# Expert rows summed in HBM by accumulating DMAs from POOL, combine stages that read the sums, and first gathers issued in the router stage

## The reference, cut to what matters

```python
# block 1
for e in range(N_EXPERTS):
    hid = jax.nn.silu(t @ w_gate[e]) * (t @ w_up[e])
    out = out + combine[:, e:e + 1] * (hid @ w_down[e])
x = x + gate2 * out
# block 2, for the tokens `toks` of expert e
hb = x_pad[toks] @ w1[e] + b1[e]
g_part = jnp.minimum(hb[..., ::2], SWIGLU_LIMIT)
u_part = jnp.clip(hb[..., 1::2], -SWIGLU_LIMIT, SWIGLU_LIMIT)
act = g_part * jax.nn.sigmoid(SWIGLU_ALPHA * g_part) * (u_part + 1)
y = act @ w2[e] + b2[e]
out = zeros.at[slot_tok].add(y * slot_gate)
```

## Time and profile before

| | us |
|---|---|
| median of 3 runs | 2692.19 (2686.52 to 2699.84) |
| the profiled execution, its own time | 2694.49 |
| its span, first to last instruction | 2692.7 |
| router stage 1 up to the last index, starts 562, ends | 604.8 |
| expert stage 1, up to the last copy of its products | 867.0 |
| combine stage 1, starts 871.2, ends | 903.7 |
| router stage 2, up to the last index | 1617.9 |
| expert stage 2, up to the last copy of its products | 2627.5 |
| combine stage 2, starts 2631.7, ends with the span | 2692.7 |

### The profile page before, as it was taken

How to read it: one execution, slowest core, us unless ns; L and a number is a source line. 1 busy time by engine, 2 the same in 40 slices (tenths; PEclk the granted TensorE clock), 3 DMA queues, 4 the chain that set the end, 5 groups by cost and what they waited for, 6 DMA issues and landing times. The chain is left out here.

```text
span 2692.7 us, 33335 instructions
## 1 busy us (share of the span) xinstructions
PE 2428.8 (90%) x12618; PEld 1168.4 (43%) x12618; DVE 1036.6 (38%) x2285; ACT 490.2 (18%) x1140; POOL 224.4 (8%) x248
## 2 busy tenths in 40 slices
PE   7999878968886899999999978999899998999975
PEld 3445656534443455667544432333233342333323
DVE  4856564761111655467421153222122222132215
ACT  3232441021111311255111020000000000000003
POOL 0000000001101000068200001000000000000002
PEclk9997777989997999899999989999999999999995
DMA  8534302669998600010311067999999999999994
GB/s 341 217 125 174 124 1 95 256 283 368 418 384 348 229 32 4 32 63 33 116 61 47 1 265 301 413 419 419 420 418 385 417 419 419 419 418 418 419 386 162
DMA packets 144054, 691.33 MB, mean 257 GB/s; under 512 B 14860, under 2 KB 42508, under 8 KB 78344
## 3 DMA queue, kind: packets, MB, share of 16 engines
q1 hardware_dynamic: 120776, 635.19, 58.4%
q0 software_dynamic: 9376, 31.73, 3.1%
q10 hardware_dynamic: 13744, 22.30, 2.3%
HBM read 640.14 MB, written 49.02 MB: 256 GB/s over the span
## 5 line engine op out<-in xcount | busy, mean ns | idle before, releaser
L2029 PE MATMUL bank<-ring,ex_xt 128*64 128x512 f32 (+4 forms) x2240 | 359.2, 507 | 25.8 <-DMA ring<-in_up 23.3
L2029 PE MATMUL bank<-x_spare,ex_xt 128*64 128x512 f32 (+4 forms) x1504 | 270.6, 519 | 18.1 <-DMA x_spare<-in_up 17.1
L2029 PEld LDWEIGHTS bank<-ring,ex_xt 128*64 128x64 f32 (+2 forms) x2240 | 126.1, 130 | 241.6 <-issue 192.0
L2070 PE MATMUL bank<-ring,ex_at 128*32 128x256 f32 (+2 forms) x1168 | 191.8, 504 | 15.9 <-DMA ring<-in_down 13.6
L2135 ACT ACTIVATE ex_xt<-bank 128x512 f32<-128x512 f32 (+1 forms) x85 | 42.7, 526 | 827.2 <-PE bank L2010 821.6
L2029 PEld LDWEIGHTS bank<-x_spare,ex_xt 128*64 128x64 f32 (+2 forms) x1504 | 98.6, 137 | 176.6 <-issue 139.2
L1977 POOL DMA_INDIRECT ex_x<-rows,index x74 | 71.2, 962 | 1080.4 <-PE bank L2010 1055.3
L2070 PE MATMUL bank<-x_spare,ex_at 128*64 128x512 f32 (+2 forms) x720 | 134.5, 519 | 15.3 <-DMA x_spare<-in_down 14.3
L2286 DVE COPY ex_y<-bank 128x512 f32<-128x512 f32 (+1 forms) x83 | 48.2, 599 | 254.0 <-PE bank L2070 253.5
L2538 PE MATMUL bank<-hT,ring 128*128 128x512 f32 x320 | 142.5, 599 | 2.5 <-ACT hT L2588 2.5
L2070 PEld LDWEIGHTS bank<-ring,ex_at 128*32 128x32 f32 (+2 forms) x1168 | 60.5, 127 | 129.3 <-issue 106.7
(11 more groups left out here) (574 smaller groups left out, 3342.2 us busy)
## 6 DMA issues: line engine op xcount, KB each, us to landing
ring<-in_up SPq DMA_DIRECT2D x170, 1024.0 KB, 25.0
x_spare<-in_up SPq DMA_DIRECT2D x120, 1024.0 KB, 27.1
ring<-in_down SPq DMA_DIRECT2D x82, 1024.0 KB, 26.7
x_spare<-in_down SPq DMA_DIRECT2D x64, 1024.0 KB, 25.7
hT<-in_up SPq DMA_DIRECT2D x30, 1024.0 KB, 24.9
ring<-in_w_in SPq DMA_DIRECT2D x14, 2048.0 KB, 12.7
ring<-in_w_ada SPq DMA_DIRECT2D x12, 2048.0 KB, 7.8
ring<-in_w_mod SPq DMA_DIRECT2D x12, 2048.0 KB, 7.6
```

What stands on the lines that cost most here:

```text
L2029: last = nc.tensor.matmul(k.ps[up_bank(b, p, r)][g * rows:(g + 1) * rows, 0:c.stop - c.start], rows_in, w[:, c], start=kk == 0, stop=kk == ...
L2070: last = nc.tensor.matmul(out, rows_in, w[:, g * width:(g + 1) * width], start=f == 0, stop=f == FT - 1)
```

## The change

The rows of an expert are weighted when they are copied out of PSUM (a tensor_scalar in place of a copy), and POOL adds them by an indirect DMA with `compute_op=add` into a tensor of 512 rows in HBM, `sums1` or `sums2`, at the row of their token. `xs` and the 24 gathers of the combine stages go, and so do the stores by ACT and SP. The combine stages read `sums` with 4 plain DMAs of 512 KB.

```diff
-    def copy_y(b, parts, slot):
+    def weighted_y(b, parts, slot, shares):
...
-                last = dve.tensor_copy(out[:, g * 512:g * 512 + w], k.ps[y_bank(b, p, g)][:, 0:w])
+                last = dve.tensor_scalar(out[:, g * 512:g * 512 + w], k.ps[y_bank(b, p, g)][:, 0:w], shares[p], None, ALU.mult)
...
+    def send(part, out, index, done):
         groups = GROUPS[part]
+        to = sums.rearrange("r (g d) -> (r g) d", g=groups)
+        pool.indirect_dma_start(out=to, out_offset=bass.IndirectOffsetOnAxis(ap=index, axis=0), in_=out[:, 0:D // groups], in_offset=None,
+                                bounds_check=groups * T - 1, oob_is_err=False, compute_op=ALU.add).then_inc(done, 16)
...
+    def store(b):
+        pool.wait_ge(s["y_sb"], b + 1)
+        if b >= 1:
+            pool.wait_ge(y_out[slot_of(b - 1)], added(b - 1))
+        for p, part in enumerate(plan.parts(b)):
+            at_ = plan.col(b, part)
+            send(part, space("y", plan.parts(b), p, y[:, slot_of(b), :]), t["index"][:, at_:at_ + 1], y_out[slot_of(b)])
...
-    gather(0)
-    gather(1)
     for b in range(B):
         if b + 2 <= B:
             pool.wait_ge(s["x_mm"], b + 1)
             gather(b + 2)
+        if b >= 2:
+            store(b - 2)
```

```diff
+    for a in range(NA):
+        pool.tensor_scalar(share[:, a, :], k.c("slot", 0, QUARTER), flat(rest)[:, a:a + 1], t["wts"][:, a // NT, a % NT:a % NT + 1], ALU.is_equal, ALU.mult).then_inc(s["share"], 1)
+    pool.wait_ge(s["sent"], 16 * NT)
+    pool.wait_ge(s["index"], 1)
+    for b in range(2):
+        for p, part in enumerate(plan.parts(b)):
+            at_ = plan.col(b, part)
+            fetch_rows(pool, k, part, htok[:, b, 512 * p:], t["index"][:, at_:at_ + 1], x_in[b])
```

More of the change, by code:

```diff
@@ L140, in col @@
         return self.first_col[part] + self.number[self.order[b]][part]
-    def row(self, b, part):
-        rank = self.order[b]
-        return QUARTER * self.first_split[part] + ROWS[part] * self.number[rank][part]
     def up_index(self, b):
@@ L1552, in output_phase, with fetch_rows, router_phase @@
     k.end()
-def router_phase(k, name, t, w_src, n_logits, top, b_row, hier, stage, plan, gain, shift, seats, up, down, seat_in):
+def fetch_rows(pool, k, part, to, index, landed):
+    groups = GROUPS[part]
+    pool.indirect_dma_start(out=to[:, 0:D // groups], out_offset=None, in_=k.a["rows"].rearrange("r (g d) -> (r g) d", g=groups),
+                            in_offset=bass.IndirectOffsetOnAxis(ap=index, axis=0),
+                            bounds_check=groups * T - 1, oob_is_err=False).then_inc(landed, 16)
+def router_phase(k, name, t, w_src, n_logits, top, b_row, hier, stage, plan, gain, shift, seats, up, down, seat_in, x_in, htok):
     nc = k.nc
@@ L1643, in _ @@
                 last.then_inc(s["map"], 1)
+                for a in range(NA):
+                    f = dict(start=a == 0, stop=a == NA - 1)
+                    pe.wait_ge(s["share"], a + 1)
+                    for g in range(4):
+                        last = nc.tensor.matmul(k.ps[7][g * QUARTER:(g + 1) * QUARTER, 0:J], share[:, a, :], hot[:, a, :], **f)
+                last.then_inc(s["shares"], 1)
                 k.keep_warm(3, 5)
@@ L1666, in _ @@
                 act.activation(m[:], m[:], ACT.Exp).then_inc(s["exp"], 1)
+                act.wait_ge(s["shares"], 1)
+                for g in range(4):
+                    rows = slice(g * QUARTER, (g + 1) * QUARTER)
+                    act.activation(t["share"][rows, col["N"]:plan.cols], every(k.ps[7][rows, :], split["N"], 2, many)[:, :, g % 2], ACT.Copy)
+                    act.activation(t["share"][rows, 0:count["W"]], every(k.ps[7][rows, :], 0, 4, count["W"])[:, :, g], ACT.Copy)
+                act.activation(t["share"][:, col["Q"]:col["Q"] + count["Q"]], k.ps[7][:, split["Q"]:split["Q"] + count["Q"]], ACT.Copy)
             @block.vector
@@ L1820, in expert_phase @@
     rounds_before = lambda b: sum(rounds(i) for i in range(b))
-    stores = lambda b: sum(GROUPS[p] for p in plan.parts(b))
+    stores = lambda b: len(plan.parts(b))
     slot_of = lambda b: b % 2
@@ L1825, in expert_phase @@
     stored = lambda b: 16 * sum(stores(i) for i in same_slot(b))
+    added = lambda b: stored(b) + 16 * stores(b)
+    quiet = plan.big - 6
+    assert b_down is None or all(plan.parts(b) == "N" for b in range(quiet, plan.big))
     biases = gathers
@@ L2079, in x_block @@
                         pe.wait_ge(s["y_sb"], 1)
+                    if b_down is not None and b == plan.big:
+                        pe.wait_ge(s["shifted"], KT)
                     transpose_x(b, parts_of(b), slot_of(b))
@@ L2109, in _ @@
                     up_block(b)
+                    if b_down is not None and quiet <= b < plan.big - 1:
+                        down_bias(b - quiet - 1)
                     x_block(b + 1)
@@ L2174, in turned @@
                     copy_a(b, parts_of(b))
-                def store(b):
-                    act.wait_ge(s["y_sb"], b + 1)
-                    for p, part in enumerate(plan.parts(b)):
-                        rows, w = ROWS[part], D // GROUPS[part]
-                        to = k.a["xs"][plan.row(b, part):plan.row(b, part) + rows, :]
-                        out = space("y", plan.parts(b), p, y[:, slot_of(b), :])
-                        for g in range(GROUPS[part]):
-                            act.dma_start(to[:, g * w:(g + 1) * w], out[g * rows:(g + 1) * rows, 0:w]).then_inc(y_out[slot_of(b)], 16)
                 act.wait_ge(s["x_mm"], 1)
@@ L2357, in _ @@
             def _(sp):
-                if b_down is not None:
-                    sp.dma_start(bd[:], b_down).then_inc(s_bd, 16)
+                for i in range(NT):
+                    sp.dma_start(acc[:, i, :], sums[i * P:(i + 1) * P, :]).then_inc(got[i], 16)
                 if keep:
-                    sp.wait_ge(got[SEATS // 2], landed(SEATS // 2))
                     k.send_pieces(sp, keep)
```

266 lines of the change are left out of this document (121 added, 145 removed).

## The result

The changed kernel takes 2742.0 us (median of 4 runs, 2736.6 to 2743.8) against 2692.7 us (4 runs, 2686.5 to 2699.8) for the kernel before: a ratio of 1.018, 95% interval 1.0155 to 1.021, 49 us slower. I had predicted 2666 us and a range of 2631 to 2706. The size, the sign and the range were all missed.

A forecast was written before the change was run, and what follows sets the result against it. DMA engines were taken to bound the expert stages, chains of short steps the combine stages. Terms -27 - 10 + 4.5 + 2.5 + 2.3 + 1 = -26.7 us gave 2666 us, range 2631 to 2706.

The forecast's parts named there:

- What bounds the kernel: Expert stages: DMA engines are the bound, shares 0.96 and 0.99; combine stages: a chain of short steps, no engine full.
- The combine stages: Shorter chains without gathers and down bias: -27 us in combine stage 2, -10 us in combine stage 1.
- the half clock: Combine stage 2: PE granted 1.2 GHz through most of it, a gain of 25.8 us; full clock would gain 30.5.
- The accumulations in turn: Expert stages: each accumulation waits for the landing of the one before; counted as nothing.
- c: Expert stages: DMA price of an accumulated row in plain stores, taken as 2: two reads and a write.
- Rival 2: Expert stage 1: accumulations in turn set the pace, +51 us, halved to +25, total 2691 us; chance 0.17.
- DMA time in the expert stages: Both expert stages: only taken slots move, additions cost two stores; stage 1 -8, stage 2 +10, together +2.3 us.
- rival 4: Expert stages: empty slots are moved all the same, +17 us, total 2683 us; chance 0.05.
- rival 1: Expert stages: the add is nearly free, destination read beside the transfer, total 2631 us; chance 0.17.
- rival 3: Expert stages: accumulating packets hold the DMA engines while reading HBM, 2735 us at four stores' price; chance 0.13.
- The hand-overs and the routers: Expert-to-combine hand-overs +4.5 us, for the last accumulation's landing; router stages +2.5 us, for added POOL, PE and ACT work.
- The early gathers: Router 2 into expert stage 2: first rows gathered ahead of the barrier win back 2.8 of 4.2 us.

The follow-up runs named there:

- the experiment: Changed kernel with the first two blocks' rows gathered at the start of the expert stage again, as in the kernel before: 2739.8 us against 2742.

## Why the prediction was wrong, step by step

**What bounds the kernel.** Right for the kernel before, and stage 2 behaved by it. In stage 1 the change itself moved the bound, from the DMA engines to a chain of landings.

**The combine stages.** Right: -29.4 and -9.8 against -27 and -10. In combine 2 I had leaned to the half clock; the granted clock was 1.00 from 2713 to 2728.7 us and 0.67 in the 10 us behind it, nearer to the other end of my bounds (-30.5).

**The accumulations in turn: this is the step that failed.** I wrote "just below the block. I count nothing, and make it a rival". The term stood at nothing, and expert stage 1 became 45.2 us longer, 36 of them by the turns. The nearest row was a gather under load, 7.0 us, and a block 7.8 us; I held the median of the cheaper kind of DMA against a threshold 0.8 us above it. I also left out POOL's way from a landing to the next issue, 0.8 us: with it even the gather's 7.0 us fill the block, and plain stores in turn do cost 15 us. The same prediction put c at 2, two reads for one, which should have made me expect a longer landing than the gather's, and it was: 8.5 us, a turn of 9.1 us. Two steps of one prediction did not speak to each other. Rival 2 was the mechanism, with its place (DVE waiting for `y_out`, PE for rows behind it) as written. Its size was not: I halved it, since the weights would run ahead, the queues empty and landings come down towards 3 us. The weights did run ahead, and where the queues were empty the landings did fall, to 4.9 us in the hole and 3.8 us at the end. But in the 200 us of 643 to 763 and 823 to 903 us the DMA share stayed at 0.97 and 1.01, and the landing at 8.5 and 8.6 us. So the brake acted in two short stretches only, and the halving was the error. My full figure of +51 us is near the +53 that stands between -8 and +45, in part by luck: taking the turns away gave back only 36 us.

**DMA time in the expert stages.** c was the number that I called the most open, and it was right: 2.1. Stage 2 grew by 13.8 us where I had 11, and shrank by 21.7 us for c = 1 where I had 22.6. Empty slots are skipped, so rival 4 is out; rival 1 (the add nearly free) and rival 3 (the packets hold the engines) are out with c = 2.1. In stage 1, though, my -8 did not come even without turns: 263.8 us is +9. By the kernel with plain stores and no turns (249.0, -5.6 against the -20 of my own formula for c = 1) about 15 us of DMA time taken away did not become time. The share there was below that of before (0.92 against 0.97 between first transposes and last rows), so the DMA engines were no longer alone at the bound. At most some 3.5 us of it are the seats in `hT`; the rest is open.

**The hand-overs and the routers.** +13.7 and +11.9 us against +4.5 and +2.5. I priced the barrier at 1.2 us, as it stands in the rows of before, where POOL is not the last to come. The price of POOL coming last stood in the instruction records of the kernel before, at the ends of its expert stages: a DRAIN of 2.83 and of 3.65 us behind POOL's last gather, hidden only because POOL was done early. I had not looked there. In router 2 I had POOL's gathers issued by 1621.6, which is 3.7 us after the last index; it was 6.1 us after, with the DRAIN behind them. PE stood idle for 3.2 us, and its clock fell from 1.00 to 0.57 and 0.66 in the products behind, so that six of them took 4.5 instead of 2.8 us. The early gathers hid 2.8 us by my sum and nothing that can be seen by the experiment.

**The rest.** The bias in stage 2 is free (999.9 against 1002.7 us without it), I had +1. The smaller clearing of HBM showed no gain that stands out of the 13 us by which the front part varies.

## What to carry to other kernels

Where each block's DMA must land before the next one's may start, the loop's length is the larger of the block and the turn, which is the landing and the issuer's way to the next issue: compare the landing of that very kind of DMA under that load with the block. Here 8.5 + 0.8 us against 7.8 us had to be counted at full price, and against 31 us cost nothing. Two targets used in turn remove the wait for one more pass over the results, but ask first whether the part of the gain that needs no accumulation (here the bias) can be had alone. And an indirect DMA that POOL issues last in a stage is paid twice, once for its landing and once for POOL's DRAIN ahead of the barrier. The price of an engine coming last can be read in the kernel before, in a stage where that engine comes early.

## What the runs showed of the hardware that I had not expected

- POOL's DRAIN at the end of a program with indirect DMAs took 2.8 to 5.5 us once the last of them had landed, gather, store or addition alike, and 6.8 to 7.0 us behind the plain stores of stage 2. Where the program did not wait for the landing, it ended 5.4 and 5.6 us after the last issue had ended in the two expert stages, and 4.5 and 1.4 us after it in the routers of the changed kernel. The barrier's own DRAIN takes 0.1 us in all of them. In router 2 of the kernel before, where POOL had issued no DMA in the stage, the DRAIN at the end of its program ended 0.1 us after POOL's last instruction.
- An adding indirect DMA occupies POOL for 1.58 us against 1.03 us for a plain one with the same rows and indices.
- Landings of an addition follow the load of the DMA engines: in stage 1 8.5 us at a share of 0.97, 4.9 us in the hole (0.25 and 0.49), 3.8 us at the end of the stage (0.10); in stage 2 9.7 us at 0.99, where plain stores land in 7.0 us.
- Transposing and weighting in one product with a diagonal matrix costs PE 0.23 us for 128x128 at the full clock, a plain transpose 0.14 us (eight in 1.09 us): four products in place of one transpose were dearer than DVE's three additions.
